# Two transformer blocks on one core: nine mixer splits moved to GpSimd, the compression cut in three, the output norm's gate product moved ahead of its root

## The chip, the core and the metric

The kernel runs on one core of a Trainium2 chip. TensorE multiplies matrices into PSUM, VectorE (DVE) and ScalarE (ACT) do elementwise work on SBUF and PSUM, GpSimd (POOL) does elementwise work on SBUF and issues some transfers, SyncE (SP) issues the weight stream. Each has its own queue, worked off in order, and waits for the others by semaphores. The metric is the device time of one execution in microseconds (us).

## What is computed

Two blocks of two layers each on a sequence of 256 tokens and a width of 1024. The first has feed-forward, attention (forgetting, then dilated), feed-forward. The second, where the change lies, has for each of its two layers:

```python
h = rms_norm_2(x, norm_mix_pre[l])
z = h @ w_in[l]
za, zq, zkv, zg, zc, zd = jnp.split(z, offsets, axis=-1)
y_conv = conformer_conv(za, ...)          # 31 taps, layer norm, silu
y_nsa  = nsa_attention(q, kv..., gates, ...)   # keys compressed, selected, windowed
y_sgu  = spatial_gating(zc, ...)
y_pool = multiscale_pool(zd, ...)
y = jnp.concatenate([y_conv, y_nsa, y_sgu, y_pool], axis=-1) @ w_out[l]
x = x + rms_norm_2(y, norm_mix_post[l])
h = rms_norm_2(x, norm_ffn_pre[l])
y = conv_ffn(h, ffn_up[l], ffn_conv_w[l], ffn_conv_b[l], ffn_down[l])
x = x + rms_norm_2(y, norm_ffn_post[l])
```

The compression inside `nsa_attention` takes blocks of 32 tokens: `gelu(blocks @ w1) @ w2`, with `w1` of 32*64 rows, for keys and for values.

## The kernel before

**Precision and weights.** Every large product is done in three matmuls of a reduced fp32 format: low part of the activations by high part of the weights, high by low, high by high (L478 to L480 in the mixers). Weights come in quarters of 128 x 1024 from a stream into a ring of four slots of two quarters. ScalarE copies a quarter to `w_hi` (L1137), which rounds it; the difference `ring - w_hi` is written over the ring as `ring_lo`. This subtraction is the split. DVE does it (L1615), all but for the list `POOL_Q`, in which before the change only one quarter of four in the feed-forwards behind the mixers stands; those GpSimd does (L406). Before each quarter TensorE waits, in `low_part`, on `w_lo_ready` (DVE's) or on `w_lo_pool` (GpSimd's).

**A mixer** uses 24 quarters: 16 for `z`, in four column groups of four quarters (`part(s, r)` is quarter 4s + r), and 8 for the output product (`out_chunk`, then `down_last`, which ends with the last three tiles and first waits for the convolution, `conv_out`). All the small work stands between them, in an order written out by hand for each engine; DVE and ScalarE have `split(...)` calls between their other steps. The steps that the prediction names:

- *Compression* (`compress`, L966): 32 positions for keys and for values, each a product of a 64x64 weight by 15 columns. It needs the blocks `blk`, which DVE makes by two additions of SBUF tiles (L2271) from the transposed keys (`qkT`, copied by ScalarE at L1486). Behind it come eight transposes (L938), quarter 12, and `compressed` (L975), which waits for ScalarE's gelu of the result (L1495, L1496).
- *Convolution*: 31 taps on DVE, SBUF to SBUF (L2238, L2241), in pieces between the other steps; then mean, variance, a reciprocal (L2353), a product of two SBUF tiles (L2356), silu on ScalarE (L1535), the high part (L1537), and on DVE the low part (L2359).
- *Attention*: ScalarE's exponentials (L1461), DVE's row sums' reciprocals (L2221, L2223) and its copy of the transposed probabilities (L2230, L2231), then TensorE's `values` (L1033).
- *Gating*: DVE's layer norm, L2311 to L2327; L2322 scales (tensor_scalar), L2325 and L2327 are products of SBUF tiles.

**Output norm.** `post_norm` on ScalarE squares the product, still in PSUM, tile 0 whole and tile 1 in two halves (L1545, L1550, L1554), and takes roots. `update_normed` on DVE waits for the root, inverts it (L1803), forms `ps * rstd * gate` (L1807) and adds it to x (L1810). The next norm's scaling (L1627) stands right behind in DVE's queue, and TensorE's transposes (L609) wait for it. After the last feed-forward the output is stored instead.

In the rows, `arena` is a large shared buffer, `ps` PSUM, `h_both` the high and low parts of the activations.

## Time and profile before

| | us |
|---|---|
| median of 3 runs | 1903.3 |
| lowest and highest run | 1901.71, 1905.03 |
| span of the profiled execution | 1901.7 |
| TensorE busy | 1805.5 |
| DVE busy | 1466.5 |
| ScalarE busy | 1049.8 |
| GpSimd busy | 131.0 |

The span is the profiled execution's own time, from its first to its last instruction. TensorE's matmuls overlap, and a busy TensorE also counts time at half clock. Start times in the rows are us from the start of the span. "Idle before" in brackets is the time that the engine stood still before the instruction, and the arrow names what ended it. Where an `x8` stands, several instructions are merged, and the time is that of them all.

### The profile page before, as it was taken

The numbers are of one execution on the slowest core, as the hardware profiler recorded it, in microseconds if no ns is written. First come the engines' busy times: TensorE is split into PE (matmuls) and PEld (weight loads), VectorE is DVE, ScalarE is ACT, GpSimd is POOL, SyncE is SP. The second block draws the span as 40 slices with busy tenths as digits, with TensorE's granted clock in tenths as the row PEclk, the third lists the DMA queues.
The fourth block names the chain that finished last, engine by engine and source line by source line (L and its number), as shares of the span: only waits on it lengthen the run. The fifth ranks groups of instructions, "written<-read, shape, count | busy, mean of one in ns | idle before, by whom it ended". The sixth has DMA issues, their size and how long they took to land.

```text
span 1901.7 us, 28364 instructions
## 1 busy us (share of the span) xinstructions
PE 1805.5 (95%) x9730; PEld 1512.8 (80%) x9730; DVE 1466.5 (77%) x2300; ACT 1049.8 (55%) x1594; POOL 131.0 (7%) x170
## 2 busy tenths in 40 slices
PE   5999899899999999999999999999889998979998
PEld 4888677688888887788878798878678887768886
DVE  6888788688888888868665576658869976878994
ACT  5554465465536553555454465545676645666663
POOL 1101010000010000000000000000012200002210
PEclk9999999899999999999999999999999999999999
DMA  9878665367888777444540164545145554324553
GB/s 384 339 274 313 236 232 210 113 220 277 279 305 287 276 278 271 165 179 176 180 151 1 64 243 176 194 177 193 67 180 191 184 194 160 112 89 169 185 193 117
DMA packets 63778, 382.04 MB, mean 201 GB/s; under 512 B 7153, under 2 KB 7409, under 8 KB 27586
## 3 DMA queue, kind: packets, MB, share of 16 engines
q1 hardware_dynamic: 42912, 300.96, 43.9%
q0 software_dynamic: 20208, 78.79, 11.5%
q10 hardware_dynamic: 578, 1.22, 0.2%
q8 instruction: 50, 0.82, 0.2%
q14 instruction: 30, 0.25, 0.0%
HBM read 379.90 MB, written 1.05 MB: 200 GB/s over the span
## 4 chain that ended last, share of the span: by engine, by line
PE 74%; DVE 14%; issue 6%; ACT 4%; DVEq 1%; DMA 1%; SPq 0%; ACTq 0%
PE ps L561 18%; PE ps L478 11%; PE ps L480 10%; PE ps L479 10%; PE ps L563 9%; DVE ring_lo L1615 3%; DVE wb L1914 2%; PE ps L843 1%; PE ps L582 1%; PE ps L584 1%; PE ps L583 1%; PE ps L609 1%; PE ps L869 1%; DVE wa L1903 1%; PE ps L856 1%
## 5 line engine op out<-in xcount | busy, mean ns | idle before, releaser
L1615 DVE TENSOR_TENSOR ring_lo<-ring,w_hi 128x1024 fp32r<-128x1024 f32 x534 | 666.5, 1265 | 257.5 <-ACT w_hi L1137 255.8
L1137 ACT ACTIVATE w_hi<-ring 128x1024 fp32r<-128x1024 f32 x556 | 579.1, 1057 | 458.7 <-PE ps L480 282.2
L561 PE MATMUL ps<-h_both,w_hi 128*128 128x512 f32 x1984 | 698.5, 397 | 0.0
L563 PE MATMUL ps<-h_both,ring_lo 128*128 128x256 f32 x1984 | 557.3, 281 | 0.0
L561 PEld LDWEIGHTS ps<-h_both,w_hi 128*128 128x128 f32 x1984 | 373.1, 188 | 89.0
L563 PEld LDWEIGHTS ps<-h_both,ring_lo 128*128 128x128 f32 x1984 | 375.8, 189 | 0.0
L478 PE MATMUL ps<-w_hi,h_both 128*128 128x512 f32 x580 | 236.8, 408 | 12.5 <-DVE h_both L2099 6.4
L480 PE MATMUL ps<-w_hi,h_both 128*128 128x512 f32 x580 | 230.2, 397 | 0.0
L479 PE MATMUL ps<-ring_lo,h_both 128*128 128x512 f32 x580 | 230.1, 397 | 0.0
L478 PE MATMUL ps<-w_hi,hid_lo 128*128 128x512 f32 x456 | 180.3, 395 | 1.3 <-DVE ring_lo L1615 1.3
L480 PE MATMUL ps<-w_hi,hid_hi 128*128 128x512 f32 x456 | 177.6, 389 | 0.0
L479 PE MATMUL ps<-ring_lo,hid_hi 128*128 128x512 f32 x456 | 177.5, 389 | 0.0
L478 PEld LDWEIGHTS ps<-w_hi,h_both 128*128 128x128 f32 x580 | 111.5, 192 | 40.1 <-issue 6.7
L480 PEld LDWEIGHTS ps<-w_hi,h_both 128*128 128x128 f32 x580 | 111.3, 192 | 24.2
L479 PEld LDWEIGHTS ps<-ring_lo,h_both 128*128 128x128 f32 x580 | 111.6, 192 | 21.7
L1652 DVE CUSTOM_DVE_ANT_0 arena<-arena 128x1024 f32<-128x1024 f32 x94 | 114.1, 1218 | 10.2 <-ACT arena L1564 7.5
L415 POOL DMA_DIRECT2D arena<-in_mod x128 | 67.8, 530 | 640.3 <-DVE arena L1652 363.4
L478 PEld LDWEIGHTS ps<-w_hi,hid_lo 128*128 128x128 f32 x456 | 85.6, 188 | 22.1 <-issue 4.4
L479 PEld LDWEIGHTS ps<-ring_lo,hid_hi 128*128 128x128 f32 x456 | 85.6, 188 | 18.6 <-issue 1.4
L480 PEld LDWEIGHTS ps<-w_hi,hid_hi 128*128 128x128 f32 x456 | 85.6, 188 | 17.9
L1251 ACT ACTIVATE wa<-ps 128x512 f32<-128x512 f32 x80 | 43.5, 596 | 71.7 <-PE ps L563 71.7
L1914 DVE SCALAR_TENSOR_TENSOR wb<-wa,cols,wb 128x254 f32<-128x254 f32 (+1 forms) x176 | 77.5, 508 | 6.6 <-ACT wb L1285 6.6
(362 smaller groups left out, 2161.7 us busy)
## 6 DMA issues: line engine op xcount, KB each, us to landing
ring<-in_stream SPq DMA_DIRECT2D x276, 1024.0 KB, 4.8
arena<-in_mod POOLq DMA_DIRECT2D x128, 512.0 KB, 5.6
arena<-in_mod SPq DMA_DIRECT2D x14, 512.0 KB, 13.4
gate<-in_wide POOLq DMA_DIRECT2D x3, 1536.0 KB, 10.3
arena<-in_nsaw POOLq DMA_DIRECT2D x2, 1072.0 KB, 8.7
ring<-in_stream SPq DMA_DIRECT2D x4, 512.0 KB, 14.9
arena<-in_konst POOLq DMA_DIRECT2D x1, 1295.5 KB, 8.4
arena<-in_mixw POOLq DMA_DIRECT2D x2, 576.0 KB, 9.6
```

Source lines behind the costliest of these rows:

```text
L415: pool.dma_start(mring[:, r, :], a["mod"][q, :, r * QUARTER:(r + 1) * QUARTER]).then_inc(mod_in[r], 16)
L478: nc.tensor.matmul(dst, x_lo, hi, start=first(i), stop=False)
L479: nc.tensor.matmul(dst, x_hi, lo, start=False, stop=False)
L480: mm = nc.tensor.matmul(dst, x_hi, hi, start=False, stop=last(i))
L561: nc.tensor.matmul(ps[:, banks[b], :].rearrange("p (w t) -> p w t", w=2), hi, h_both[:, :, 2 * r + i, :], start=(r == 0 and i == 0), stop= ...
L563: mm = nc.tensor.matmul(ps[:, banks[b], T:2 * T], lo, h_hi[:, 2 * r + i, :], start=False, stop=(r == 3 and i == 1))
L582: nc.tensor.matmul(dst, x_lo, hi, start=False, stop=False)
L1137: nc.scalar.activation(w_hi[:, q % SPLITS, :], ring[:, half % SLOTS, (q % 2) * QUARTER:(q % 2 + 1) * QUARTER], ACT.Copy).then_inc(w_hi_rea ...
L1251: nc.scalar.activation(wa[:, n * 512:(n + 1) * 512].rearrange("p (b t) -> p b t", b=2), low, ACT.Copy).then_inc(low_kept, 1)
L1615: v.tensor_tensor(ring_lo[:, slot, cs], ring[:, slot, cs], w_hi[:, q % SPLITS, :], ALU.subtract).then_inc(w_lo_ready, 1)
L1652: return v.tensor_tensor_reduce(out=junk[n % 2], in0=src, in1=crow, scale=1.0, scalar=0.0, op0=ALU.mult, op1=ALU.add, accum_out=to)
L1914: ins = v.scalar_tensor_tensor(out=acc[:, c, lag:T], in0=wa[:, c * T:(c + 1) * T - lag], scalar=w, in1=acc[:, c, lag:T], op0=ALU.mult, op1 ...
```

## The change

Three things. First, the quarters 6, 8, 10, 12, 14, 16, 18, 20 and 22 of each mixer are split by GpSimd and no more by DVE; GpSimd does the nine in a row between its transfers. Second, the compression is cut in three pieces of 11, 11 and 10 positions, which stand behind quarters 9, 10 and 11 and no more all behind 11. Third, `update_normed` multiplies by the gate as soon as the square is there, and multiplies by the inverse root while it adds to x; the number of DVE instructions over the data stays the same. Two semaphores are also merged into one (`silu_c_ready`), and ScalarE signals its squares on a semaphore of their own.

```diff
-POOL_Q = [BASE[_f] + 4 * _j + 5 for _f in ("ffn4", "ffn5") for _j in range(UPS)]
+MIX_POOL = (6, 8, 10, 12, 14, 16, 18, 20, 22)
+POOL_Q = [q for _l in range(LAYERS) for q in [BASE[f"mix{_l}"] + _k for _k in MIX_POOL] + [BASE[f"ffn{4 + _l}"] + 4 * _j + 5 for _j in range(UPS)]]
...
+            def mix_split(l):
+
+                for k in MIX_POOL:
+                    q = BASE[f"mix{l}"] + k
+                    pool.wait_ge(w_hi_ready, q + 1)
+                    slot, cs = (q // 2) % SLOTS, slice((q % 2) * QUARTER, (q % 2 + 1) * QUARTER)
+                    nc.gpsimd.tensor_tensor(ring_lo[:, slot, cs], ring[:, slot, cs], w_hi[:, q % SPLITS, :], ALU.subtract).then_inc(w_lo_pool, 1)
...
             wide(6, 0, 3).then_inc(gate_in, 16)
+            mix_split(0)
             pool.wait_ge(x_ready, 14)
...
             split(4)
+            mix_split(1)
             split(5)
...
-                def compress():
+                def compress(first, end):
                     pe.wait_ge(blk_ready, l + 1)
                     pe.wait_ge(cv_ready, l + 1)
-                    for e in range(CMP_LEN):
+                    for e in range(first, end):
...
                 part(2, 1, bD)
+                compress(0, 11)
                 part(2, 2, bD)
+                compress(11, 22)
                 part(2, 3, bD)
-                compress()
+                compress(22, CMP_LEN)
...
-                tick.mark(nc.scalar.activation(xn[:, 0, :], psf[:, o:o + D], ACT.Square, scale=D ** -0.5, accum_out=ms[:, 2:3]))
-                tick.settle()
+                nc.scalar.activation(xn[:, 0, :], psf[:, o:o + D], ACT.Square, scale=D ** -0.5, accum_out=ms[:, 2:3]).then_inc(y_squared, 1)
+                act.wait_ge(y_squared, 3 * k + 1)
...
+            def update_normed(k, s):
 
                 w = (wa, wb)
...
+                def gained(tt, lo, hi):
+                    o = (DOWN_BANK + 2 * tt) * 512
+                    tick.mark(v.tensor_tensor(w[tt][:, lo:hi], psf[:, o + lo:o + hi], gate[:, s, lo:hi], ALU.mult))
+
+                def root(tt):
                     dve.wait_ge(yms_ready, 2 * k + tt + 1)
                     tick.mark(v.reciprocal(rstd[:, 2 + tt:3 + tt], rms[:, 2 + tt:3 + tt]))
...
+                def added(tt, lo, hi):
+                    v.scalar_tensor_tensor(out=x[:, tt, lo:hi], in0=w[tt][:, lo:hi], scalar=rstd[:, 2 + tt:3 + tt], in1=x[:, tt, lo:hi],
+                                           op0=ALU.mult, op1=ALU.add).then_inc(x_half if hi == 512 else x_ready, 1)
+
+                dve.wait_ge(y_squared, 3 * k + 1)
+                gained(0, 0, D)
+                root(0)
+                added(0, 0, D)
+                dve.wait_ge(y_squared, 3 * k + 2)
+                gained(1, 0, 512)
+                dve.wait_ge(y_squared, 3 * k + 3)
+                gained(1, 512, D)
+                root(1)
+                added(1, 0, 512)
+                added(1, 512, D)
```

TensorE in a mixer, around the compression, before: the last matmuls of quarter 11, the block, the transposes, and the start of quarter 12.

```order
L479 MATMUL ps<-ring_lo,h_both 128x512
L480 MATMUL ps<-w_hi,h_both 128x512
L966 MATMUL ps<-arena 64x15 [waits cv_ready,blk_ready]
L966 MATMUL ps<-arena 64x15 x63
L938 MATMUL ps<-konst,arena 128x128 [waits rot_ready]
L938 MATMUL ps<-konst,arena 128x128 x7
L478 MATMUL ps<-w_hi,h_both 128x512 [waits w_lo_ready]
```

And now, from the end of quarter 9 to the start of quarter 12 (L489 to L491 are the old L478 to L480, L977 the old L966, L949 the old L938):

```order
L491 MATMUL ps<-w_hi,h_both 128x512
L977 MATMUL ps<-arena 64x15 [waits cv_ready,blk_ready]
L977 MATMUL ps<-arena 64x15 x21
L489 MATMUL ps<-w_hi,h_both 128x512 [waits w_lo_pool]
...
L977 MATMUL ps<-arena 64x15 [waits cv_ready,blk_ready]
L977 MATMUL ps<-arena 64x15 x21
L489 MATMUL ps<-w_hi,h_both 128x512 [waits w_lo_ready]
...
L977 MATMUL ps<-arena 64x15 [waits cv_ready,blk_ready]
L977 MATMUL ps<-arena 64x15 x19
L949 MATMUL ps<-konst,arena 128x128 [waits rot_ready]
L949 MATMUL ps<-konst,arena 128x128 x7
```

The wait for the blocks has moved ahead by two quarters, and quarter 10 now waits for GpSimd.

DVE in a mixer, from the rotary products to the block additions, before:

```order
L2261 TENSOR_TENSOR wa<-arena 128x384 [waits c_copied]
L2261 TENSOR_TENSOR wa<-arena 128x384
L1615 TENSOR_TENSOR ring_lo<-ring,w_hi 128x1024 [waits w_hi_ready]
L2264 TENSOR_TENSOR wb<-arena 128x384
L2264 TENSOR_TENSOR wc<-arena 128x384
L1615 TENSOR_TENSOR ring_lo<-ring,w_hi 128x1024 [waits w_hi_ready]
L2271 TENSOR_TENSOR arena<-arena 128x240 [waits qkT_ready]
L2271 TENSOR_TENSOR arena<-arena 128x240
```

And now (L2289, L2292, L2299 are the old L2261, L2264, L2271, L1628 is the old L1615):

```order
L2289 TENSOR_TENSOR wa<-arena 128x384 [waits c_copied]
L2289 TENSOR_TENSOR wa<-arena 128x384
L2292 TENSOR_TENSOR wb<-arena 128x384
L2292 TENSOR_TENSOR wc<-arena 128x384
L1628 TENSOR_TENSOR ring_lo<-ring,w_hi 128x1024 [waits w_hi_ready]
L2299 TENSOR_TENSOR arena<-arena 128x240 [waits qkT_ready]
L2299 TENSOR_TENSOR arena<-arena 128x240
```

The split of quarter 10 is gone from between the rotary products; that of quarter 11 is left.

DVE at a mixer's end, from the convolution's product to the update of x, before:

```order
L2356 TENSOR_TENSOR arena<-arena,wb 128x512 [waits cd_ready,dve_tick]
L1615 TENSOR_TENSOR ring_lo<-ring,w_hi 128x1024 [waits w_hi_ready]
L2359 TENSOR_TENSOR h_both<-hT,h_both 128x512 [waits conv_hi]
L1615 TENSOR_TENSOR ring_lo<-ring,w_hi 128x1024 [waits w_hi_ready] x2
L1803 RECIPROCAL rstd<-rms 128x1 [waits yms_ready,gate_in]
L1807 SCALAR_TENSOR_TENSOR wa<-ps,rstd,gate 128x1024 [waits dve_tick]
L1810 TENSOR_TENSOR x<-x,wa 128x1024 [waits dve_tick]
L1803 RECIPROCAL rstd<-rms 128x1 [waits yms_ready]
L1807 SCALAR_TENSOR_TENSOR wb<-ps,rstd,gate 128x512 [waits dve_tick]
L1810 TENSOR_TENSOR x<-x,wb 128x512 [waits dve_tick]
L1807 SCALAR_TENSOR_TENSOR wb<-ps,rstd,gate 128x512 [waits dve_tick]
L1810 TENSOR_TENSOR x<-x,wb 128x512 [waits dve_tick]
```

And now (L2384 and L2387 are the old L2356 and L2359):

```order
L2384 TENSOR_TENSOR arena<-arena,wb 128x512 [waits cd_ready,dve_tick]
L2387 TENSOR_TENSOR h_both<-hT,h_both 128x512 [waits conv_hi]
L1628 TENSOR_TENSOR ring_lo<-ring,w_hi 128x1024 [waits w_hi_ready] x2
L1817 TENSOR_TENSOR wa<-ps,gate 128x1024 [waits y_squared,gate_in]
L1821 RECIPROCAL rstd<-rms 128x1 [waits yms_ready]
L1825 SCALAR_TENSOR_TENSOR x<-wa,rstd,x 128x1024 [waits dve_tick]
L1817 TENSOR_TENSOR wb<-ps,gate 128x512 [waits y_squared] x2
L1821 RECIPROCAL rstd<-rms 128x1 [waits yms_ready]
L1825 SCALAR_TENSOR_TENSOR x<-wb,rstd,x 128x512 [waits dve_tick]
L1825 SCALAR_TENSOR_TENSOR x<-wb,rstd,x 128x512
```

The split of quarter 22 is gone, and the products with the gate stand ahead of the reciprocals and wait for the squares alone.

## Rows read from the trace of the kernel before

**Rows 1.** The page, part 4: shares of the chain that ended last.

```profile
PE 74%; DVE 14%; issue 6%; ACT 4%; DVEq 1%; DMA 1%; SPq 0%; ACTq 0%
```

**Rows 2.** Stages (us; busy us by engine, counts; PEclk, DMA share, GB/s); timeline of TensorE.

```profile
1400.00:1404.00 4.00, 4.00 (x19) 3.75 (x18) 3.58 (x8) 3.16 (x7) 0.48 (x1) 0.50 0.97 331
...
1283.35 2.29 PE L609 MATMUL ps<-konst,xn 128*128 128x128 f32 x16 [2.11 <-DVE xn L1627]
```

**Rows 3.** Timeline of TensorE, first mixer (start us, us, instruction, idle before, releaser).

```profile
1319.59 4.33 PE L966 MATMUL ps<-arena 64*64 64x15 f32 x128
1323.86 1.97 PE L938 MATMUL ps<-konst,arena 128*128 128x128 f32 x8
1325.48 0.77 PE L478 MATMUL ps<-w_hi,h_both 128*128 128x512 f32 x1
...
1330.36 0.29 PE L975 MATMUL ps<-arena 64*64 64x15 f32 x4
...
1330.79 0.50 PE L478 MATMUL ps<-w_hi,h_both 128*128 128x512 f32 x1
...
1333.73 0.49 PE L1004 MATMUL ps<-arena 64*128 64x256 f32 x2
```

**Rows 4.** Timelines of ScalarE, first mixer, and of TensorE, second mixer.

```profile
1330.11 0.18 ACT L1496 ACTIVATE arena<-ps 64x15 f32<-64x15 f32 x1
...
1639.66 0.29 PE L975 MATMUL ps<-arena 64*64 64x15 f32 x4 [0.89 <-ACT arena L1496]
```

**Rows 5.** Timelines of GpSimd and DVE in the first feed-forward behind a mixer.

```profile
1432.74 3.16 POOL L406 TENSOR_TENSOR ring_lo<-ring,w_hi 128x1024 fp32r<-128x1024 f32 x1 [8.68 <-ACT w_hi L1137]
...
1454.93 2.41 POOL L406 TENSOR_TENSOR ring_lo<-ring,w_hi 128x1024 fp32r<-128x1024 f32 x1 [8.68 <-ACT w_hi L1137]
...
1433.79 5.16 DVE L1914 SCALAR_TENSOR_TENSOR wb<-wa,cols,wb 128x255 f32<-128x255 f32 x8 [0.16 <-ACT wb L1285]
...
1454.60 1.28 DVE L1903 TENSOR_TENSOR wa<-ps,wa 128x512 f32<-128x512 f32 x2
1455.80 2.62 DVE L1615 TENSOR_TENSOR ring_lo<-ring,w_hi 128x1024 fp32r<-128x1024 f32 x1
```

**Rows 6.** Timelines of ScalarE and DVE, w_hi of quarter 12 and the blocks.

```profile
1312.21 1.05 ACT L1137 ACTIVATE w_hi<-ring 128x1024 fp32r<-128x1024 f32 x1
...
1313.40 1.05 DVE L2271 TENSOR_TENSOR arena<-arena 128x240 f32<-128x240 f32 x2
```

**Rows 7.** Timelines of ScalarE, DVE and TensorE around the split of quarter 18.

```profile
1352.67 1.04 ACT L1137 ACTIVATE w_hi<-ring 128x1024 fp32r<-128x1024 f32 x1
...
1357.28 0.19 ACT L1461 ACTIVATION_READ_ACCUMULATOR arena<-arena,nmax 128x1 f32 x1
...
1355.04 0.69 DVE L2325 TENSOR_TENSOR wb<-wb,arena 128x512 f32<-128x512 f32 x1
...
1356.38 1.22 DVE L1615 TENSOR_TENSOR ring_lo<-ring,w_hi 128x1024 fp32r<-128x1024 f32 x1
...
1359.15 0.65 PE L1033 MATMUL ps<-arena 128*64 128x256 f32 x2 [0.96 <-DVE arena L2231]
```

**Rows 8.** Timelines of ScalarE, DVE and TensorE around the split of quarter 22.

```profile
1382.00 1.05 ACT L1137 ACTIVATE w_hi<-ring 128x1024 fp32r<-128x1024 f32 x1
...
1383.92 0.69 DVE L2356 TENSOR_TENSOR arena<-arena,wb 128x512 f32<-128x512 f32 x1
...
1387.18 0.50 PE L582 MATMUL ps<-w_hi,h_both 128*128 128x512 f32 x1 [1.47 <-DVE h_both L2359]
```

**Rows 9.** Timelines of ScalarE, DVE and TensorE, first output norm and what follows.

```profile
1394.94 0.19 ACT L1554 ACTIVATION_READ_ACCUMULATOR xn<-ps 128x1 f32 x1
...
1395.49 0.16 DVE L1803 RECIPROCAL rstd<-rms 128x1 f32<-128x1 f32 x1 [0.86 <-ACT rms L1556]
...
1397.87 0.69 DVE L1810 TENSOR_TENSOR x<-x,wb 128x512 f32<-128x512 f32 x1
...
1399.21 3.67 PE L609 MATMUL ps<-konst,xn 128*128 128x128 f32 x16 [4.80 <-DVE xn L1627]
```

More of the change, by code:

```diff
@@ L1796, in update @@
                     v.tensor_tensor(x[:, tt, lo:hi], x[:, tt, lo:hi], w[tt][:, lo:hi], ALU.add).then_inc(x_half if hi == 512 else x_ready, 1)
[L1798 removed]
+            def update_normed(k, s):
                 w = (wa, wb)
[L1801 removed]
+                def gained(tt, lo, hi):
+                    o = (DOWN_BANK + 2 * tt) * 512
+                    tick.mark(v.tensor_tensor(w[tt][:, lo:hi], psf[:, o + lo:o + hi], gate[:, s, lo:hi], ALU.mult))
+                def root(tt):
                     dve.wait_ge(yms_ready, 2 * k + tt + 1)
                     tick.mark(v.reciprocal(rstd[:, 2 + tt:3 + tt], rms[:, 2 + tt:3 + tt]))
[L1804 to L1810 removed]
+                    tick.settle()
+                def added(tt, lo, hi):
[12 more added lines that the diff above has]
+                added(1, 512, D)
             def ffn(f):
```

33 lines of the change are left out of this document (12 added, 21 removed).

## The prediction

> **What bounds the kernel now.** I read the chain of work that ended last first, to see which engine sets the end [rows 1]. TensorE has 74% of it, DVE 14%, ScalarE 4%. So DVE time is worth something only where TensorE waits for it. The next view is the timeline of TensorE, DVE and ScalarE in the two mixers (1280 to 1398 us, 1594 to 1706 us), read for idle time of TensorE and its releaser. The two mixers repeat each other within 0.1 us at most places, so each term below is worked out on the first one and taken twice. Last come the stretches where the granted clock is 0.50, that is 1.2 instead of 2.4 GHz [rows 2], and the places where GpSimd and DVE already work at once [rows 5].
>
> **Compression in three pieces.** It is 64 small products, in the profile 128 records, in one block of 4.33 us. After it TensorE runs at half clock: the eight transposes behind it take 1.97 us, the quarter after them 4.88 us (1325.48 to 1330.36), where the next quarter takes 2.94 us (1330.79 to 1333.73) [rows 3]. Cut into pieces of some 1.5 us with quarters of 2.7 us between, I take it that the clock stays at 2.4 GHz. The transposes then take half, which gives 1.0 us. The quarter would give another 1.94 us, but that isn't got: TensorE waits next for the hidden column of the compression, and ScalarE reaches it by a chain that starts at the transposes' end, from 1325.83 [rows 3] to 1330.29, back to back, 4.46 us [rows 4]. Before, TensorE came to that point just then; in the second mixer it already waited 0.89 us there [rows 4]. So the quarter's gain turns into idle time. Two more switches between small and wide products cost about 0.1 us each. Term 1: -0.8 us a mixer, -1.6 in all; between 0 (the clock falls all the same) and -1.2 each.
>
> **Nine quarters split on GpSimd.** The split on GpSimd takes 2.41 us [rows 5] where DVE takes 1.22 [rows 7]. Each starts when ScalarE has made w_hi, and TensorE needs the result at least 3 us later at all nine, so none is late by itself. What DVE is spared is 9 x 1.14 us (a split less its overlap with the next). Where does this reach TensorE? Nowhere that I can find. The one removed split that lies in the chain is that of quarter 18, and DVE's next step behind it needs ScalarE's exponentials, whose last read ends at 1357.47 [rows 7], and the split ends at 1357.60. The gain of the whole part is thus zero, and what is left is its price.
>
> The price is in [rows 5]. A DVE subtraction of two SBUF tiles that started at 1455.80, while GpSimd's was running from 1454.93, took 2.62 us. GpSimd ended at 1457.34, and 1457.34 + 1.08 is the end of DVE's: it stood still until GpSimd was through. The addition from PSUM at 1454.60 (two in 1.28 us) was not held up. The other way round, GpSimd's at 1432.74 came while a DVE subtraction was under way and took 3.16 us, and the DVE group behind it 5.16 us. So a DVE instruction with two SBUF inputs and a split on GpSimd exclude each other for the whole of one of them, and one with a PSUM input goes on. The Trainium skill says the same (SBUF — State Buffer, Who interferes with whom): a DVE instruction with two SBUF inputs contends with a GpSimd instruction that reads SBUF, and the other side fully blocks. It is a rule against this change: by it the DVE steps named below pay; without it terms 2 to 4 would be zero and the sum -6.0 us. The trace agrees, with the 2.62 us.
>
> I went through the nine places with the times of before.
> - Quarters 6, 8, 14, 16: DVE is idle or works from PSUM while GpSimd runs. Zero. Quarter 20 holds up two pairs of convolution taps by 0.9 us, which have 2 us of room before TensorE asks for them. Zero.
> - Quarters 10 and 12, term 2. Quarter 10's split runs across DVE's first convolution taps and puts its rotary products off by some 0.8 us; the split that DVE is spared behind them (1.14) makes that good, and the blocks for the compression, two additions of SBUF tiles at 1313.40 [rows 6], come at about 1313.1. The first piece of the compression now asks for them two quarters earlier than before: 1319.59 less two quarters of some 2.8 us, about 1313.9. Quarter 12's w_hi is ready at 1313.27 [rows 6], between the two additions. If GpSimd gets its turn there, it works from about 1313.5 to 1315.9, the second addition ends at 1316.4, and TensorE stands for 2.5 us in a stretch where it had no idle time. Behind the waiting TensorE instruction stands all the rest of the mixer. If DVE keeps its turn between two instructions that are queued without a wait, it is 0.1 us. No row shows GpSimd waiting before two such instructions; the nearest is that of 1432.74, where it started as the running subtraction ended, but DVE had nothing ready then. I take 2.4 us each, 4.8 in all; ends 0.1 and 2.7 each.
> - Quarter 18, term 3. w_hi is ready at 1353.71, GpSimd works from about 1354.1 to 1356.5. DVE's layer norm of the gating has two products of SBUF tiles, the first at 1355.04 [rows 7]; it now starts at 1356.5. The two products end 1.4 us later, the spared split takes 1.1 us of it back: +0.3 us. Should the tensor_scalar pair ahead be held up too, it is +1.1. DVE then copies the probabilities, for which TensorE already waited 0.96 us at 1359.15 [rows 7]. I take 0.7 each, 1.4 in all.
> - Quarter 22, term 4. w_hi is ready at 1383.05 [rows 8]; GpSimd works to 1385.46. The convolution's product of two SBUF tiles, due at 1383.92, is held up by 1.54 us. Behind it in DVE's queue stands the low part of the convolution, and for that TensorE waits (1.47 us at 1387.18, [rows 8]). The split that is spared lay in DVE's idle time. Both events hang on the same ScalarE step, so they meet whatever comes before. 3.1 us in all; ends 0 and 1.6 each.
>
> **Gate ahead of the root.** After the last output half is squared (1395.13) DVE waited for the root and then did root and four halves of arithmetic, 1395.49 to 1398.56, of which 0.2 is the reciprocal and 0.72 each half [rows 9]. Now two of the four are products with the gate, of which one is done while the square is taken, and one after 1395.13: 0.72 + 0.2 + 2 x 0.72 = 2.36, so the end is 1397.5, 1.07 us earlier. Three times the next norm stands behind it (TensorE idle 4.80 us, [rows 9]), whose DVE part is in queue right behind; the fourth time the output's transfer does. The renaming of semaphores costs nothing. Term 5: 4 x -1.1 = -4.4 us; ends -0.6 (ScalarE's part of the next norm is late) and -1.2 each.
>
> **The clock elsewhere**, term 6. Behind each of the three norms TensorE starts at half clock and is still there four us later [rows 2]. A gap shorter by 1.1 us may shorten that stretch (-1.5 us each: three us of it at full speed) or only move work into it (+0.5 each). A longer idle time in terms 2 and 4 may bring a new one. I take zero, and keep the ends.
>
> **The sum**: -1.6 + 4.8 + 1.4 + 3.1 - 4.4 = +3.3 us. The profiled execution's span of 1901.7 is near the fastest of the three runs; the difference is put on the median, 1903.3, which gives 1906.6 us.
>
> **The rivals.** *DVE keeps its turn*: GpSimd doesn't get between the two queued additions; term 2 is 0.2 in all. For it: they are queued with no wait. Against: GpSimd started the moment a running one ended. Sum -1.3, 1902.0 us.
> *The shorter gaps bring the clock back*: as that rival, and behind the three norms the low stretch is shorter, 3 x -1.5. For it: at 1283 us, behind a gap of 2.11 us, the 16 transposes took 2.29 us and not 3.67 [rows 2, 9]. Against: a gap of 3.7 us is still long. 1897.5 us, the faster side.
> *A stall that costs the clock*: 2.5 us of idle time right before a piece of small products is what a low stretch looks like. If TensorE falls to 1.2 GHz there, the quarter behind it takes 4.88 for 2.94 us as in [rows 3], 1.94 us more in each mixer: 1910.5 us, and 1914 if the 3 us ahead of the last tiles does it too. For it: in the first mixer the clock fell behind the block of small products. Against: idle times of 0.9 and 1.8 us in the mixers left it alone. With the clock kept at 2.4 GHz behind both stalls the rival is dead; with one fall it decides for slower. This is the slower side.
> That the change doesn't do what it says I give no chance: GpSimd's queue has no transfer to wait for inside a mixer.
>
> **How the numbers follow.** Forecast 0.38 (1903 to 1910 by its own ends), DVE keeps its turn 0.20, clock back 0.20, stall and clock 0.22. A measurement can tell about 0.2% from no change, 3.8 us: under 1899.5 or over 1907.1. The forecast lies near the upper edge and gives 0.16 to slower, 0.22 to same; the second gives 0.17 to same, the third 0.17 to faster, the fourth 0.21 to slower: faster 0.20, same 0.43, slower 0.37. The range 1897 to 1912 holds the first three and most of the fourth.
>
> **What would show it.** Right, if TensorE waits over 2 us for the block additions before the first piece; if DVE's convolution product before the last tiles takes over 2 us; if TensorE waits 1.5 us for the hidden column; if the gap before the norms' transposes is 3.7 us and the clock holds at 1.0 through the compression. Wrong, if GpSimd's splits and DVE's two-SBUF instructions run side by side, if GpSimd's quarter 12 takes over 3 us (then it gave way), or if the low stretches behind the norms are gone.

## The result and the profile after

| | us |
|---|---|
| changed kernel, median of 8 runs | 1909.39 (1906.29 to 1911.54) |
| kernel before, median of 8 runs | 1903.05 (1901.33 to 1906.39) |
| ratio | 1.0030, 95% interval 1.0019 to 1.0042 |
| span of the profiled execution | 1907.2 (before 1901.7) |

The change makes the kernel slower by about 0.3%, some 6 us. The forecast of 1906.6 us is 2.8 us below, and the range held the time. The way to it was wrong in three places (terms 1, 2 and 6), and their errors cancelled in part, so that the number came close is partly luck.

First the page of the changed kernel, parts 1, 4 and 5: busy time, the chain that ended last, and DVE's group of splits.

```profile
PE 1811.8 (95%) x9730; PEld 1512.6 (79%) x9730; DVE 1466.0 (77%) x2282; ACT 1049.1 (55%) x1594; POOL 176.8 (9%) x188
...
PE 74%; DVE 13%; issue 6%; ACT 5%; DVEq 1%; DMA 1%; SPq 0%; ACTq 0%
...
L1628 DVE TENSOR_TENSOR ring_lo<-ring,w_hi 128x1024 fp32r<-128x1024 f32 x516 | 644.8, 1267 | 254.1 <-ACT w_hi L1150 252.1
```

DVE has 18 splits fewer, worth 22 us, and is as busy as before (1466.5 then). The time it was spared came back as time in which it stood blocked: the same instructions took 22 us longer (the convolution's taps 5.8, the step behind the block additions 4.3, the tensor_scalar pairs of the gating 3.6 and of the gates 3.5, the convolution's product 2.9, taps of the feed-forward 1.9). GpSimd took 46 us more. The chain is that of [rows 1] within one point.

**Compression.** The timeline of TensorE in the first mixer answers to [rows 3]:

```profile
1313.27 1.46 PE L977 MATMUL ps<-arena 64*64 64x15 f32 x44
1317.64 1.46 PE L977 MATMUL ps<-arena 64*64 64x15 f32 x44
...
1322.01 1.34 PE L977 MATMUL ps<-arena 64*64 64x15 f32 x40
1323.28 1.09 PE L949 MATMUL ps<-konst,arena 128*128 128x128 f32 x8
...
1328.89 0.29 PE L986 MATMUL ps<-arena 64*64 64x15 f32 x4 [1.75 <-ACT arena L1509]
...
1330.03 0.63 PE L490 MATMUL ps<-ring_lo,h_both 128*128 128x512 f32 x1
...
1333.80 0.49 PE L1015 MATMUL ps<-arena 64*128 64x256 f32 x2
```

The pieces and the transposes run at full speed (1.09 us where it was 1.97). No idle time stands before the first piece, so term 2 isn't there. Before the hidden column TensorE waits 1.75 us, as I had said. But behind that wait the products take 0.63 us apiece instead of 0.39. The quarter runs at 1.2 GHz, as before the change, and the scores start at 1333.80, where they started at 1333.73, although this execution had reached the mixer 0.9 us earlier. The low stretch has moved behind the idle time.

**The blocks.** GpSimd and DVE around quarters 10 and 12 answer to [rows 6]:

```profile
1305.70 2.55 POOL L420 TENSOR_TENSOR ring_lo<-ring,w_hi 128x1024 fp32r<-128x1024 f32 x1 [3.52 <-ACT w_hi L1150]
...
1305.11 3.82 DVE L2269 SCALAR_TENSOR_TENSOR arena<-arena,cols 128x256 f32<-128x256 f32 x4
...
1311.86 1.06 DVE L2299 TENSOR_TENSOR arena<-arena 128x240 f32<-128x240 f32 x2
1312.84 2.67 DVE L2302 TENSOR_TENSOR arena<-wa 128x384 f32<-128x384 f32 x1
...
1312.44 2.66 POOL L420 TENSOR_TENSOR ring_lo<-ring,w_hi 128x1024 fp32r<-128x1024 f32 x1 [4.19 <-ACT w_hi L1150]
```

GpSimd's quarter 12 starts 0.1 us after the second of the two additions has begun (1311.86 + half of 1.06 is about 1312.4), is held up by it (2.66 us for some 2.4) and then blocks the next DVE step, for which nobody waits. Quarter 10 was served in the middle of four DVE instructions that stood queued without a wait, which answers the question of who gets the turn: GpSimd does (the group took 1.67 us before).

**Quarters 18 and 22**, GpSimd, DVE and TensorE; they answer to [rows 7, 8]:

```profile
1353.85 2.59 POOL L420 TENSOR_TENSOR ring_lo<-ring,w_hi 128x1024 fp32r<-128x1024 f32 x1 [10.80 <-ACT w_hi L1150]
...
1354.35 2.57 DVE L2350 TENSOR_SCALAR wb<-wa,arena 128x256 f32<-128x256 f32 x2
1356.95 0.69 DVE L2353 TENSOR_TENSOR wb<-wb,arena 128x512 f32<-128x512 f32 x1
...
1382.33 2.40 POOL L420 TENSOR_TENSOR ring_lo<-ring,w_hi 128x1024 fp32r<-128x1024 f32 x1 [9.29 <-ACT w_hi L1150]
...
1383.12 2.15 DVE L2384 TENSOR_TENSOR arena<-arena,wb 128x512 f32<-128x512 f32 x1
...
1387.84 0.80 PE L593 MATMUL ps<-w_hi,h_both 128*128 128x512 f32 x1 [2.92 <-DVE h_both L2387]
```

At quarter 18 DVE's pair of tensor_scalar is held up too (2.57 us, 0.73 before), and at quarter 22 its product, as the prediction has it: TensorE waits 2.92 us for the last tiles instead of 1.47.

**The clock behind that wait**, busy time by stage (us, busy us by engine with counts, PEclk, DMA share, GB/s):

```profile
1388.00:1390.00 2.00, 2.00 (x5) 1.62 (x6) 1.96 (x2) 1.98 (x3) 0.00 (x0) 0.50 0.00 0
1390.00:1392.00 2.00, 2.00 (x6) 1.52 (x6) 0.40 (x1) 0.46 (x2) 0.00 (x0) 0.50 0.03 8
1392.00:1394.00 2.00, 2.00 (x7) 1.52 (x6) 0.00 (x0) 0.63 (x1) 0.00 (x0) 0.50 0.00 0
```

The granted clock is 0.50 here, 1.2 GHz. From the first of the last tiles to the next norm's transposes it takes 13.58 us (1387.84 to 1401.42) where a mixer at full speed with the same norm takes 10.85 us (below). That is 2.73 us, and 2.68 in the second mixer, the largest single loss in this execution.

**The norm**, TensorE in the timeline; it answers to [rows 9]:

```profile
1401.42 1.97 PE L620 MATMUL ps<-konst,xn 128*128 128x128 f32 x8 [3.62 <-DVE xn L1640]
```

The gap is 3.62 us instead of 4.80.

### The profile page after: what moved, and what is told of

Same layout as the page of the kernel before. It is cut to its first block, busy times and chain, and to the rows that moved or that the text cites. A ratio compares the mean times of both kernels' runs of the same rounds, so it can differ in the third digit from the quotient of the medians.

```text
span 1907.2 us, 28368 instructions
## 1 busy us (share of the span) xinstructions
PE 1811.8 (95%) x9730; PEld 1512.6 (79%) x9730; DVE 1466.0 (77%) x2282; ACT 1049.1 (55%) x1594; POOL 176.8 (9%) x188
## 3 DMA queue, kind: packets, MB, share of 16 engines
q10 hardware_dynamic: 578, 1.22, 0.2%
## 4 chain that ended last, share of the span: by engine, by line
PE 74%; DVE 13%; issue 6%; ACT 5%; DVEq 1%; DMA 1%; SPq 0%; ACTq 0%
PE ps L572 17%; PE ps L489 11%; PE ps L491 11%; PE ps L490 10%; PE ps L574 9%; DVE ring_lo L1628 3%; DVE wb L1942 2%; PE ps L593 1%; PE ps L594 1%; PE ps L595 1%; PE ps L854 1%; DVE wa L1931 1%; PE ps L880 1%; PE ps L867 1%; ACT w_hi L1150 1%
## 5 line engine op out<-in xcount | busy, mean ns | idle before, releaser
L1628 DVE TENSOR_TENSOR ring_lo<-ring,w_hi 128x1024 fp32r<-128x1024 f32 x516 | 644.8, 1267 | 254.1 <-ACT w_hi L1150 252.1
L489 PE MATMUL ps<-w_hi,h_both 128*128 128x512 f32 x580 | 238.4, 411 | 12.5 <-DVE h_both L2127 6.4
L491 PE MATMUL ps<-w_hi,h_both 128*128 128x512 f32 x580 | 230.4, 397 | 0.0
L489 PE MATMUL ps<-w_hi,hid_lo 128*128 128x512 f32 x456 | 180.3, 395 | 1.3 <-DVE ring_lo L1628 1.2
L491 PE MATMUL ps<-w_hi,hid_hi 128*128 128x512 f32 x456 | 177.6, 389 | 0.0
L489 PEld LDWEIGHTS ps<-w_hi,h_both 128*128 128x128 f32 x580 | 111.5, 192 | 40.5 <-issue 7.1
L491 PEld LDWEIGHTS ps<-w_hi,h_both 128*128 128x128 f32 x580 | 111.7, 193 | 24.8
L489 PEld LDWEIGHTS ps<-w_hi,hid_lo 128*128 128x128 f32 x456 | 85.6, 188 | 21.8 <-issue 4.3
L491 PEld LDWEIGHTS ps<-w_hi,hid_hi 128*128 128x128 f32 x456 | 85.6, 188 | 18.0
```

The source lines that it names most:

```text
L489: nc.tensor.matmul(dst, x_lo, hi, start=first(i), stop=False)
L491: mm = nc.tensor.matmul(dst, x_hi, hi, start=False, stop=last(i))
L1628: v.tensor_tensor(ring_lo[:, slot, cs], ring[:, slot, cs], w_hi[:, q % SPLITS, :], ALU.subtract).then_inc(w_lo_ready, 1)
```

## The experiments

Each kernel was timed beside the kernel before on the same chip. Two things are needed to read them. First, executions of one kernel scatter with a standard deviation of some 2 us, and in most of these kernels the longer executions are those with the lower mean granted clock. The 33 runs of before in the first set lie between 1897.76 and 1906.79 us, and their time and mean clock have a correlation of -0.74, so about half of the variance goes with the clock. So a single trace tells exactly what happened in it, but where the low-clock stretches fell is that execution's.

Second, the feed-forwards behind the mixers run at one of two paces, with a granted clock of 1.00 at both: 20 products of the first part take 3.47 or 3.53 us. In the changed kernel's profile the first of them has the faster pace (290 products in the 50 us from 1450) and the second the slower (285 in the 50 us from 1730). The slower one makes a feed-forward some 2.2 us longer. It came in 11 of the 28 feed-forwards of the profiles, in seven kernels' first and four kernels' second, those with the splits alone and with the gate alone among them, and no run shows what sets it. So the whole times of two single profiles are not compared here without looking where the difference lies.

To compare traces I took five intervals between starts on TensorE that occur in all of them (first and second mixer, us, worked out from the timelines):

| kernel | norm to hidden column | to scores | to third output chunk | to last tiles | to next transposes |
|---|---|---|---|---|---|
| before | 47.01, 47.89 | 3.37, 3.37 | 36.56, 36.56 | 16.89, 15.30 | 12.03, 12.03 |
| changed | 46.44, 47.56 | 4.91, 4.91 | 37.27, 37.27 | 16.77, 16.77 | 13.58, 13.53 |
| changed, again | 46.44, 48.21 | 3.39, 4.97 | 37.29, 37.29 | 18.36, 18.23 | 10.85, 10.87 |
| gate alone | 47.02, 47.66 | 3.38, 3.37 | 36.56, 37.06 | 16.91, 15.34 | 10.84, 10.83 |
| pieces alone | 46.73, 47.86 | 3.38, 3.38 | 36.56, 36.56 | 15.28, 15.30 | 12.03, 12.03 |
| splits alone | 46.81, 47.95 | 3.38, 3.42 | 37.29, 37.30 | 18.35, 16.77 | 12.02, 13.55 |

The changed kernel stands in it twice. Where two entries of one design differ by 0.5 us or more, the longer holds a stretch at 1.2 GHz that another wait didn't hide. The rest repeats within 0.1 us.

### The gate alone

In outline, not the kernel's own lines:

```diff
-    v.scalar_tensor_tensor(out=w, in0=psf, scalar=rstd, in1=gate, op0=mult, op1=mult)
-    v.tensor_tensor(x, x, w, add)
+    v.tensor_tensor(w, psf, gate, mult)          # while the root is formed
+    v.scalar_tensor_tensor(out=x, in0=w, scalar=rstd, in1=x, op0=mult, op1=add)
```

> The kernel before with the gate ahead of the root alone: no split on GpSimd, compression in one block. The prediction's term 5: four times -1.1 us, so -4.4 us against the kernel before, the gap before the transposes of each norm 3.7 us instead of 4.80, and the same low-clock stretch behind it. Rival (what the trace of the changed kernel suggests): the gap shrinks by 1.2 us and the low stretch behind it is shorter too (16 transposes in 3.3 instead of 3.7 us, and full speed some 3 us earlier), so -6 to -8 us.

Measured: 1897.25 us against 1902.24, ratio 0.9977 (0.9966 to 0.9987), so -4.4 us (-6.5 to -2.5). Last tiles to next transposes: 10.84 instead of 12.03 us. The transposes and the first feed-forward product behind them then take 3.57 instead of 3.36 us, since they now wait for the norm's parts; at the kernel's end the arithmetic behind the last product takes 3.35 instead of 4.54 us. Three times 0.98 and once 1.19 make 4.1 us. Term 5 stands, and the rival's further gain isn't seen, though the interval's end of -6.5 touches it.

### The pieces alone

```diff
                 part(2, 1, bD)
+                compress(0, 11)
                 part(2, 2, bD)
+                compress(11, 22)
                 part(2, 3, bD)
-                compress()
+                compress(22, CMP_LEN)
```

> The kernel before with the compression in three pieces alone. The prediction's term 1: the clock stays at 2.4 GHz behind the pieces and TensorE waits some 1.7 us for the hidden column, -0.8 us a mixer, -1.6 us in all. Rival: the clock falls right behind that wait, so that the quarter after it takes 4.4 instead of 2.9 us; the slow stretch has only moved, and the scores start no earlier than before: 0 to +2 us in all.

Measured: ratio 1.0005 (0.9988 to 1.0021). In the profiled execution the clock held behind the hidden column in both mixers (3.38 us), and even so the hidden column came only 0.28 us earlier (46.73 for 47.01). The twelve runs fall into two groups, 1897.66 to 1900.51 us at a mean clock of 0.984 to 0.988, and 1906.63 to 1910.69 us at 0.978 to 0.983. So neither theory has it: the fixed gain is a third of what I took. The longer group goes with a lower clock, but no profile shows one of its executions, and two falls behind the hidden column (1.5 us each) would be 3 us of the 8 or 9 between the groups; the rest stays open.

One row bears on what the splits are worth. TensorE, pieces alone:

```profile
1314.61 1.46 PE L977 MATMUL ps<-arena 64*64 64x15 f32 x44 [0.25 <-DVE arena L2284]
```

TensorE waits for the blocks ahead of the first piece. With the nine splits taken from DVE this wait is gone, and the hidden column comes at 46.44 instead of 46.73 us.

### The nine splits alone

```diff
-POOL_Q = [BASE[_f] + 4 * _j + 5 for _f in ("ffn4", "ffn5") for _j in range(UPS)]
+MIX_POOL = (6, 8, 10, 12, 14, 16, 18, 20, 22)
+POOL_Q = [q for _l in range(LAYERS) for q in [BASE[f"mix{_l}"] + _k for _k in MIX_POOL] + [BASE[f"ffn{4 + _l}"] + 4 * _j + 5 for _j in range(UPS)]]
```

> The kernel before with the nine splits on GpSimd alone. By the blocked DVE instructions alone (terms 3 and 4, term 2 at zero as in the trace of the changed kernel) +0.7 and +1.45 us a mixer, +4.3 us in all, clock 1.0 through the last tiles of the mixers. Rival, the stall that costs the clock: the idle time before the last tiles grows to 2.9 us and the clock falls behind it, +2.7 us a mixer more, +9.8 us in all.

Measured: 1907.69 us, ratio 1.0033 (1.0022 to 1.0044), +6.3 us (+4.2 to +8.4). Quarter 18 costs 0.73 and quarter 22 1.47 us a mixer, as in the changed kernel. The clock fell behind the last tiles' wait in the second mixer (13.55) and not in the first (12.02), where it had fallen behind the third output chunk's wait (18.35). The time lies between the two expectations.

### Quarter 22 back on DVE

```diff
-MIX_POOL = (6, 8, 10, 12, 14, 16, 18, 20, 22)
+MIX_POOL = (6, 8, 10, 12, 14, 16, 18, 20)
```

> The changed kernel with quarter 22 split on DVE again (eight of 24 on GpSimd). If the lock alone counts, the idle time before the last tiles goes back from 2.9 to 1.5 us: -1.45 us a mixer against the changed kernel, -2.9 in all, so +3.4 us against the kernel before. If the longer idle time is also what makes the clock fall, the last tiles run at 2.4 GHz again: -1.45 and -2.7 us a mixer, -8.4 us in all, so about -2 us against the kernel before.

Measured: 1904.42 us, ratio 1.0010 (1.0002 to 1.0019), +1.9 us against before. Against the changed kernel's +5.7 us that is -3.8 us; the two were not on the same chip, and the intervals allow 1 to 7 us. The wait is 1.47 us again and the stretch behind it ran at full speed both times (10.85). That is nearer to the lock alone (DVE held up by the split, -2.9) than to lock and clock at their full price (-8.4). But against the changed kernel's second measurement (+9.1, next section) it is -7.2, so this run doesn't choose between the two. It shows that the wait goes back.

### The changed kernel once more

> The changed kernel itself once more, beside the three others and on their chip: a second profile of it. If the low-clock stretches stand at fixed places, they are again behind the hidden column and before the last tiles of both mixers (4.91 us to the scores, 13.5 us from the last tiles to the next transposes). If they are a matter of the single execution, some of them are gone and the rest of the trace agrees within 0.1 us.

Measured: 1910.84 us, ratio 1.0048 (1.0034 to 1.0061). The second profile settles how the first is to be read. The waits of TensorE are the same within 0.02 us (where no low stretch hides one), the low stretches are not at the same places. TensorE in the timeline:

```profile
1389.51 0.50 PE L593 MATMUL ps<-w_hi,h_both 128*128 128x512 f32 x1 [2.92 <-DVE h_both L2387]
```

The stages from there (columns as above):

```profile
1389.00:1391.00 2.00, 1.49 (x6) 1.06 (x7) 1.75 (x3) 1.98 (x3) 0.00 (x0) 1.00 0.01 4
1391.00:1393.00 2.00, 2.00 (x10) 1.66 (x10) 1.07 (x1) 1.45 (x3) 0.00 (x0) 1.00 0.04 8
```

The same 2.92 us of idle time, and the clock stays at 2.4 GHz. In this execution it had fallen earlier, behind the third output chunk's wait (18.36 and 18.23 us to the last tiles, not 16.77). That wait of 1.71 us stands in the kernel before too, and there too the clock fell behind it in the first mixer (TensorE; 0.39 us is a product at 2.4 GHz):

```profile
1370.29 0.52 PE L478 MATMUL ps<-w_hi,h_both 128*128 128x512 f32 x1 [1.71 <-DVE h_both L2344]
...
1371.46 0.63 PE L478 MATMUL ps<-w_hi,h_both 128*128 128x512 f32 x1
```

### Products in the idle time before the last tiles

```diff
                 for kk in tail:
                     if late is not None and kk == late[0]:
+                        for _ in range(8):
+                            nc.tensor.matmul(ps[:, 7, :], h_hi[:, 4, 0:P], h_hi[:, 4:6, :].rearrange("p c t -> p (c t)"), start=True, stop=True)
                         pe.wait_ge(late[1], late[2])
```

> The changed kernel with eight more products of 128x512 on TensorE, into a bank that nobody reads any more, ahead of the wait for the convolution's low part in each mixer; the output is the same. The eight take some 1.8 us, so of the 2.92 us of idle time some 1.1 is left; the last tiles start no earlier. If the long idle time is what lets the clock fall, the last tiles run at 2.4 GHz in both mixers: from their first product to the next norm's transposes 10.8 instead of 13.5 us, and 3.5 to 5.4 us less than the changed kernel. Rival: the fall has nothing to do with the idle time; then the low stretch stays and the time is that of the changed kernel.

Measured: 1906.33 us, ratio 1.0025 (1.0012 to 1.0038), beside 1.0048 of the changed kernel on the same chip: -4.5 us by the medians. Timeline of TensorE:

```profile
1383.26 1.97 PE L600 MATMUL ps<-h_both 128*128 128x512 f32 x8
```

The stages from there:

```profile
1386.00:1388.00 2.00, 1.66 (x7) 1.23 (x8) 1.75 (x3) 1.98 (x3) 0.00 (x0) 1.00 0.02 4
1388.00:1390.00 2.00, 2.00 (x9) 1.62 (x10) 0.90 (x1) 1.45 (x3) 0.00 (x0) 1.00 0.04 8
```

Both mixers take 10.85 us from the last tiles to the transposes. But so did both mixers of *the changed kernel once more*, without the products, and the two profiles agree throughout: first mixer 116.32 us (116.33 there), feed-forward 191.32 (191.31), second mixer 119.58 (119.57). The 5.3 us by which this profile is shorter lie ahead of the first mixer (3.2) and behind the second (2.1, the feed-forward's faster pace), where nothing was edited. So the timed runs say that the kernel with eight more products in each mixer is probably shorter (the two intervals overlap slightly), and no trace shows that the clock behind this wait is the reason.

### Products in the idle time before the hidden column

```diff
                 def compressed():
+                    pe.wait_ge(d_copied, l + 1)
+                    for _ in range(5):
+                        nc.tensor.matmul(ps[:, bD, :], h_hi[:, 4, 0:P], h_hi[:, 4:6, :].rearrange("p c t -> p (c t)"), start=True, stop=True)
                     pe.wait_ge(hid_ready, l + 1)
```

> The changed kernel with five more products of 128x512 on TensorE ahead of the wait for the compression's hidden column (1.75 us of idle time), into a bank that is free by then; the output is the same. If the clock fell there for the idle time, the quarter behind takes 3.4 instead of 4.9 us: up to 1.5 us less a mixer, 0 to 3 us less than the changed kernel, the last tiles as in the changed kernel. Rival: low stretches come at that place with or without idle time; no difference.

Measured: 1909.80 us, ratio 1.0039 (1.0024 to 1.0053). The scores come 3.38 us behind the hidden column in both mixers, so the low stretch there is gone, and the profile has one of full price behind the last tiles' wait in both mixers (13.52, 13.52). The time isn't told apart from the changed kernel's; in this execution what was saved at one place was lost at the next.

### Quarter 10 back on DVE

```diff
-MIX_POOL = (6, 8, 10, 12, 14, 16, 18, 20, 22)
+MIX_POOL = (6, 8, 12, 14, 16, 18, 20, 22)
```

> The changed kernel with quarter 10 split on DVE again (eight of 24 on GpSimd). It tests term 2, which came out as zero: the second addition for the compression started 0.1 us before GpSimd could have taken quarter 12. With the split of quarter 10 back on DVE the two additions come some 0.3 us later. If GpSimd gets between two queued DVE instructions, it takes quarter 12 first, and TensorE waits 2.3 to 2.6 us before the first piece: +4.6 to +5.2 us against the changed kernel. Rival (DVE keeps its turn): the wait before the first piece is 0.25 us, +0.5 us in all.

Measured: 1921.54 us (1914.35 to 1927.87), ratio 1.0098 (1.0076 to 1.0121): 10.7 us more than the changed kernel on the same chip. GpSimd, DVE and TensorE in the first mixer:

```profile
1311.92 2.37 POOL L420 TENSOR_TENSOR ring_lo<-ring,w_hi 128x1024 fp32r<-128x1024 f32 x1 [10.25 <-ACT w_hi L1150]
...
1311.98 3.13 DVE L2299 TENSOR_TENSOR arena<-arena 128x240 f32<-128x240 f32 x2
...
1315.17 2.53 PE L977 MATMUL ps<-arena 64*64 64x15 f32 x44 [2.36 <-DVE arena L2299]
```

Here is the whole of term 2, as predicted for a place where it then didn't happen. GpSimd starts as DVE's split of quarter 11 (1310.85, 1.22 us) ends, ahead of the additions that stand queued behind it; these take 3.13 instead of 1.06 us, TensorE waits 2.36 us, and behind the wait the first piece takes 2.53 instead of 1.46 us, at half clock. Norm to hidden column is 51.70 and 52.79 us where it was 46.44 and 47.56. The expectation of +4.6 to +5.2 left out the clock.

### Gate and pieces

The two edits above together, no split on GpSimd.

> The kernel before with the gate ahead of the root and the compression in three pieces, no split on GpSimd. Fixed terms: -1.0 us behind each of three norms, -1.2 us at the end, -0.3 us a mixer for the pieces: -4.7 us against the kernel before. If the 1.75 us of idle time before the hidden column lets the clock fall, +1.5 us in each mixer where it does, so -4.7 to -1.7 us; the pieces are then worth nothing or less beside the gate alone (-4.4 us measured).

Measured: 1899.99 us, ratio 0.9991 (0.9982 to 1.0000), -1.7 us. With the gate alone it was 0.9977 (0.9966 to 0.9987). So the pieces bring nothing beside the gate and probably cost 2 to 3 us (the intervals just touch): in the profile of the second mixer 4.98 us lie between hidden column and scores, again behind an idle time of 1.75 us.

### Gate, and products in the norms' gaps

```diff
             def norm(m):
+                if m >= 7:
+                    for _ in range(12):
+                        nc.tensor.matmul(ps[:, 7, :], h_hi[:, 4, 0:P], h_hi[:, 4:6, :].rearrange("p c t -> p (c t)"), start=True, stop=True)
```

> The kernel before with the gate ahead of the root, and twelve more products of 128x512 on TensorE in the idle time ahead of the transposes of the last three norms, into a bank that nobody reads; the output is the same. The twelve take some 2.6 us of the 3.62. If the clock falls behind a norm for its idle time, the low stretch of 3.4 to 6.8 us behind each of the three is gone: 0.5 to 2 us less a norm than with the gate alone, -6 to -10 us against the kernel before. Rival: the low stretch has another cause, or the transposes and waits hide it: as with the gate alone, -4.4 us.

Measured: 1893.54 us, ratio 0.9958 (0.9944 to 0.9971), -8.0 us. Timeline of TensorE behind the first mixer:

```profile
1391.49 2.88 PE L623 MATMUL ps<-h_both 128*128 128x512 f32 x12
1395.28 1.11 PE L620 MATMUL ps<-konst,xn 128*128 128x128 f32 x8 [0.90 <-DVE xn L1641]
...
1398.84 0.47 PE L572 MATMUL ps<-h_both,w_hi 128*128 128x512 f32 x1 [0.93 <-DVE h_both L1659]
```

The two stages that hold the transposes and the first products of the feed-forward:

```profile
1395.00:1397.00 2.00, 1.28 (x10) 1.02 (x11) 1.56 (x5) 1.97 (x5) 1.48 (x3) 1.00 0.96 365
1397.00:1399.00 2.00, 1.07 (x9) 0.87 (x9) 2.00 (x4) 1.81 (x6) 0.00 (x0) 1.00 0.54 205
```

The same stages in the kernel with the gate alone, and its first product of the feed-forward:

```profile
1395.00:1397.00 2.00, 1.45 (x7) 1.45 (x8) 1.55 (x5) 1.94 (x6) 1.57 (x3) 0.62 0.85 332
1397.00:1399.00 2.00, 2.00 (x11) 1.82 (x9) 2.00 (x5) 1.51 (x5) 0.00 (x0) 0.53 0.83 266
...
1399.12 0.47 PE L572 MATMUL ps<-h_both,w_hi 128*128 128x512 f32 x1
```

With the products the granted clock is 1.00 through both stages, and without them 0.62 and 0.53; it stayed up behind the other two norms as well. What this brought in these two executions is less than the stages suggest: the faster transposes end in a wait for the norm's low part, and the feed-forward starts 3.56 us behind the transposes' start instead of 3.57. It is the same behind the third norm, and 1.4 us are gained behind the second. In other executions without the products the low stretch reaches further into the feed-forward (its 13th product starts 5.7 to 6.9 us behind the transposes' start), and there it costs up to 1.2 us. The interval overlaps slightly with that of the gate alone (0.9966 to 0.9987), so the further gain of 3 to 4 us is likely, its size is rough, and its place is only partly shown.

### Gate and the five splits that hold nobody up

```diff
-MIX_POOL = (6, 8, 10, 12, 14, 16, 18, 20, 22)
+MIX_POOL = (6, 8, 14, 16, 20)
```

> The kernel before with the gate ahead of the root and only the five splits on GpSimd that hold nobody up by my reckoning (quarters 6, 8, 14, 16 and 20); compression in one block. If sparing DVE these splits is worth nothing, as the prediction has it, and GpSimd's exclusion there is hidden, the time is that of the gate alone: -4.4 us against the kernel before. Rival: DVE, with 5 x 1.14 us less to do in each mixer, brings something TensorE waits for earlier: -6 us or more.

Measured: 1898.42 us, ratio 0.9974 (0.9962 to 0.9985), -4.9 us. That is the gate alone, within the interval of some 2 us. Ten splits taken from DVE bring nothing and cost nothing that can be measured here.

### Gate, pieces and products in both kinds of idle time

> The gate ahead of the root, the compression in three pieces, no split on GpSimd; and products that nobody reads on TensorE in two kinds of idle time: twelve ahead of the transposes of the last three norms, five ahead of the hidden column in each mixer. If the clock falls for idle time, the pieces now keep their gain of 0.3 us a mixer, and the time is 0.6 us below the gate with the twelve products (-8 us): -8.6 us against the kernel before. Rival: low stretches come elsewhere in the mixers for the pieces, as they did beside the gate alone (-1.7 us instead of -4.4): -5 us.

Measured: 1895.90 us, ratio 0.9963 (0.9950 to 0.9976), -7.0 us. The stage from 1100 to 1880 us:

```profile
1100.00:1880.00 780.00, 754.59 (x4215) 630.82 (x4215) 604.17 (x978) 473.71 (x758) 56.60 (x26) 1.00 0.46 168
```

The clock didn't fall once in 780 us. But the time is not below that of the kernel without pieces (0.9958), so the pieces gain nothing that can be measured, even where the clock is held. The best version here is the gate with products in the norms' gaps, 8.0 us below the kernel before, where the changed kernel is 6 to 9 above it.

## Why the prediction came out as it did

**Term 1, pieces (-0.8 us a mixer): mis-sized, and its condition failed.** "I take it that the clock stays at 2.4 GHz" held through the pieces, and the quarter's gain turned into idle time as said. Behind the one block the clock fell in 10 of 10 mixers of the five kernels that have it; through the pieces it fell in 0 of 16, where no stall stands ahead of them. The fixed gain of the edits together is 0.57 us (46.44 for 47.01): the transposes take 0.88 us less, and start 0.32 later. The pieces alone give 0.28, since the blocks then come 0.3 us too late for the first piece. What failed is the step that the clock stays up behind the new idle time of 1.75 us. It fell there in 8 of 14 mixers in the profiles that have this wait (changed 2 of 2, again 1, quarter 22 back 1, quarter 10 back 2, gate and pieces 1, products before the last tiles 1, pieces alone 0), at 1.5 us each, and in 0 of 4 with products in the gap. The pieces trade a low stretch that was nearly hidden, since the hidden column was waited for anyway, for one that isn't.

**Term 2, blocks (+2.4 us a mixer): price right, event absent.** I had reckoned that quarter 10's split would delay DVE by 0.8 us. DVE reached the additions about 0.3 us earlier than that, and the order of events turned over on 0.1 us. What I had chosen in the main question, that GpSimd gets its turn between two queued DVE instructions, is shown by the kernel with quarter 10 on DVE, where it took its turn between the split of quarter 11 and the first addition: 2.36 us where I took 2.4. The range's lower end of 0.1 covered the near miss for another reason, that DVE might keep its turn. That rival is dead, though the time of term 2 in the changed kernel is the one it gives.

**Terms 3 and 4: right, term 3 with luck.** 0.7 us taken, 0.70 to 0.73 measured; 1.54 taken, 1.45 to 1.47 measured. For quarter 18 I had priced two cases at 0.3 and 1.1 us and taken the middle. The case that came is the one of 1.1, the tensor_scalar pair held up as well, and it costs 0.7: the pair took 1.84 us longer (2.57 for 0.73), of which the spared split gives 1.14 back. The Trainium skill (SBUF — State Buffer, Who interferes with whom) and the trace agree here again; the section's full block is the whole of terms 3 and 4.

**Term 5, gate (-1.1 us each): right.** The gap shrank by 1.18 us; 0.2 of it went back behind each of the three norms, and none at the end. -4.1 us by the trace, -4.4 by the timed runs, -4.4 predicted.

**Spared DVE time at zero: nearly right.** The kernel with five harmless splits equals the gate alone within the interval. "Nowhere that I can find" missed one place, which only the pieces open: the 0.25 us for which TensorE waits ahead of the first piece when DVE still does all the splits.

**Term 6, the clock at zero: this is the step that failed.** The fixed terms as measured are 2 x (-0.57 + 0.70 + 1.47) - 3 x 0.98 - 1.19 = -0.9 us. The profiled execution is 5.5 us longer than before's, and reached the first mixer 0.9 us earlier. So some 7 us are low-clock stretches in the dense parts of the mixers: 2.73 and 2.68 behind the last tiles' waits, 1.53 twice before the scores and 1.1 in the second mixer's first part make 9.6, less the 2.5 us that before had inside its own mixers. The feed-forwards differ too, by -2.0 and +0.4 us, with the gate's gain in both and the slower pace in the second. The second execution has 6.4 in place of the 9.6, at partly other places.

So the sum of +3.3 was near the measured +5.7 (3.6 to 8.0) since 4.8 us that weren't there made up for most of the clock's loss. Of the rivals, *a stall that costs the clock* described the mechanism, at the second of the two places it named, and its 1910.5 us is the nearest of the four times to the measured one, which is luck again: it contains the 4.8 us of term 2 and a fall at the first place, and neither came. I had argued against it that "idle times of 0.9 and 1.8 us in the mixers left it alone". That was read from one execution, and not rightly even there: behind the wait of 1.71 us at 1370.29 in the first mixer the products take 0.63 us apiece, and the last tiles come 16.89 us later where they come 15.30 later in the second.

The timed kernels add up to about the same. The splits alone (+6.3) and the gate with the pieces (-1.7) make +4.6, where the changed kernel is +5.7 and +9.1 in its two measurements.

How firm is idle time as the cause? Behind the wait of 2.92 us the clock fell in 7 of 10 mixers (changed 2, again 0, splits alone 1, quarter 10 back 2, products before the hidden column 2), behind the 1.47 us of the kernels without a split of quarter 22 in 0 of 16, and behind 2.92 us filled with eight products in 0 of 2, which says little beside the 0 of 2 of the second execution. Behind the norms it fell in all 36 gaps without products and in none of 6 with them. That is the firm case. The length of the wait alone doesn't order the others:

| TensorE's wait, us | where | mixers in which the clock fell behind it |
|---|---|---|
| 1.47 | last tiles, quarter 22 on DVE | 0 of 16 |
| 1.71 | third output chunk, every kernel | 15 of 28 |
| 1.75 | hidden column, pieces | 8 of 14 |
| 1.83 | transposes 14 us behind the scores, every kernel | 4 of 28 |
| 2.11 | first mixer's first transposes, every kernel | 0 of 14 |
| 2.92 | last tiles, quarter 22 on GpSimd | 7 of 10 |
| 3.62 or 4.80 | three norms | 36 of 36 |

The Trainium skill (TensorE: Matmul & The Clock Gate, HAM oscillation — how this bites in real kernels) describes waits for data that let the array fall back, so that the next group starts cold. The trace agrees at the norms; it adds that at 1.71, 1.75 and 2.92 us it is a chance of roughly one half to two thirds and not a rule, and that behind 2.11 us it never came. Nor does it need a wait: it fell at the one block of small products, ahead of which TensorE doesn't wait. What decides it in the single execution stays open. I ran nothing that tells whether the work ahead of a wait matters beside its length.

## What to carry to other kernels

Work moved to GpSimd isn't free for DVE: list which DVE instruction with SBUF operands runs at the moment the input becomes ready, and who waits for that instruction; here two of nine places cost 2.2 us a mixer, and one of the other seven missed costing 2.4 by 0.1 us. An edit that turns TensorE's busy time into idle time can lose more by the clock than it gives, so a gain that ends in a wait should be booked at zero or with a product stream in the wait. Where a term hangs on the order of two events 0.1 us apart, give both orders their price, and read a low-clock stretch in a single profile as one draw: a second profile of the same kernel tells which parts of a trace repeat. When a kernel with an edit has the shorter profile, compare it stage by stage first: here 5.3 us of difference lay wholly where nothing had been edited.

## What the runs showed of the hardware that I hadn't expected

- GpSimd gets in between DVE instructions that are queued without a wait: quarter 10's split started in the middle of a group of four (3.82 us, 1.67 before), and in the kernel with quarter 10 on DVE the two additions took 3.13 instead of 1.06 us.
- A pair of tensor_scalar from SBUF to SBUF is held up by GpSimd's split like an instruction with two SBUF inputs: 2.57 us for two of 128x256 (0.73 before), and even four of 128x4 took 2.13 us (0.38 before).
- The low-clock stretches of one kernel stand at different places in two executions, while its waits agree within 0.02 us; mean granted clock and time have a correlation of -0.74 over 33 runs of the kernel before.
- At a granted clock of 1.00 the feed-forwards' products come at one of two paces, 20 in 3.47 or in 3.53 us, some 2.2 us over one feed-forward; the same kernel had the one in its first and the other in its second.
- TensorE products whose result nobody reads, put into its idle time ahead of the norms, go with a clock that stays up: 12 in each of three gaps of 3.6 us leave 0 falls of 6 where there are 36 of 36 without, and a ratio of 0.9958 where it is 0.9977 without them (the intervals overlap slightly); with five more per mixer before the hidden column the granted clock stayed at 1.00 for 780 us.
